# Unused unit-matrix products on TensorE at four places of a hybrid mLSTM/NSA decoder step

## The reference, cut to what matters

```python
h = rmsnorm(x, g_mix)
proj = h @ w_in + b_in
h_a, ... = mlstm_branch(...)            # chunkwise: C_new = decay * C + sum_s ws * k (x) v
o_b, ... = attend(...)                  # NSA: compressed, selected and window branch
gm = sigmoid(g_mrg)
y = gm[..., :D_MODEL] * (h_a @ w_a) + gm[..., D_MODEL:] * (o_b @ w_b)
x = x + y @ w_o
x = x + swiglu(rmsnorm(x, g_ffn), w_ffn_in, w_ffn_out)
```

## Time and profile before

| | |
|---|---|
| time, median of 3 runs | 2207.27 us (2204.72 to 2209.68) |
| time of the profiled execution | 2205.3 us |
| its span, first to last instruction | 2203.3 us |
| mean granted TensorE clock over the span | 0.96 |
| PE busy | 2016.2 us (92%) |
| DVE busy | 1045.0 us (47%) |
| ACT busy | 764.2 us (35%) |
| POOL busy | 527.9 us (24%) |

### The profile page before, as it was taken

The page is one execution under the profiler, slowest core; times in us unless marked ns, Lnnn a source line. Parts: engine busy times, 40 slices in busy tenths (PEclk is TensorE's granted clock), DMA queues, the critical chain, the costliest instruction groups (busy, mean ns, idle before and its releaser), DMA issues. The chain is left out here.

```text
span 2203.3 us, 33142 instructions
## 1 busy us (share of the span) xinstructions
PE 2016.2 (92%) x13796; PEld 1862.3 (85%) x13796; DVE 1045.0 (47%) x1752; ACT 764.2 (35%) x1435; POOL 527.9 (24%) x440
## 2 busy tenths in 40 slices
PE   4999999966888986998899999899999999999997
PEld 3999999855666763665799989899999999999997
DVE  4988863466888874314232343533343323322222
ACT  4233333443766761222222233322222224432212
POOL 2445322203654571222011112111111001111000
PEclk9999999885999986999999999999999999999999
DMA  5465531101000006354433331333323333333332
GB/s 186 126 196 170 158 122 36 40 6 39 1 1 20 1 1 224 112 171 133 153 92 96 88 101 44 94 89 87 96 85 89 96 99 98 100 108 88 87 89 66
DMA packets 258147, 203.11 MB, mean 92 GB/s; under 512 B 20342, under 2 KB 237276, under 8 KB 252687
## 3 DMA queue, kind: packets, MB, share of 16 engines
q1 hardware_dynamic: 246399, 150.92, 23.6%
q0 software_dynamic: 6144, 39.46, 5.2%
q10 hardware_dynamic: 5456, 10.62, 1.5%
HBM read 178.59 MB, written 26.54 MB: 93 GB/s over the span
## 5 line engine op out<-in xcount | busy, mean ns | idle before, releaser
L2933 DVE TENSOR_TENSOR ffn_w_l<-ffn_raw,ffn_w_h 128x1024 fp32r<-128x1024 f32 (+1 forms) x136 | 163.8, 1205 | 273.6 <-ACT ffn_w_h L2866 273.3
L98 PE MATMUL banks<-h_h,ffn_w_l 128*128 128x264 f32 x1408 | 288.3, 286 | 5.5 <-DVE ffn_w_l L2933 5.5
L98 PE MATMUL banks<-h_l,ffn_w_h 128*128 128x264 f32 x1408 | 288.2, 286 | 0.0
L98 PE MATMUL banks<-h_h,ffn_w_h 128*128 128x264 f32 x1408 | 287.9, 286 | 0.0
L2866 ACT CAST ffn_w_h<-ffn_raw 128x1024 fp32r<-128x1024 f32 (+1 forms) x136 | 138.6, 1020 | 332.2 <-PE banks L98 331.1
L98 PEld LDWEIGHTS banks<-h_h,ffn_w_l 128*128 128x128 f32 x1408 | 220.1, 189 | 6.0 <-DVE ffn_w_l L2933 5.8
L98 PEld LDWEIGHTS banks<-h_l,ffn_w_h 128*128 128x128 f32 x1408 | 219.4, 189 | 0.0
L98 PEld LDWEIGHTS banks<-h_h,ffn_w_h 128*128 128x128 f32 x1408 | 219.2, 189 | 0.0
L2854 POOL TENSOR_TENSOR act_l_rest<-ffn_act,act_h 128x528 fp32r<-128x528 f32 x38 | 71.3, 1876 | 377.3 <-ACT act_h L2874 377.3
L674 POOL TENSOR_TENSOR fm_w_l<-fm_raw,fm_w_h 128x512 fp32r<-128x512 f32 x54 | 96.5, 1788 | 218.4 <-ACT fm_w_h L731 218.4
L89 PE MATMUL banks<-fm_hT_h,fm_w_l 128*128 128x352 f32 x648 | 146.8, 335 | 0.5 <-DVE hT_l L863 0.5
(11 more groups left out here) (517 smaller groups left out, 4244.3 us busy)
## 6 DMA issues: line engine op xcount, KB each, us to landing
ffn_raw<-in_w_ffn_in_dram SPq DMA_DIRECT2D x88, 512.0 KB, 3.9
ffn_raw<-in_w_ffn_out_dram SPq DMA_DIRECT2D x32, 512.0 KB, 4.0
fm_raw<-in_w_in_dram SPq DMA_DIRECT2D x44, 256.0 KB, 3.1
early_w_raw<-in_w_in_dram SPq DMA_DIRECT2D x32, 256.0 KB, 2.9
merge_raw<-in_w_in_dram SPq DMA_DIRECT2D x32, 256.0 KB, 2.9
ffn_raw<-in_w_ffn_out_dram SPq DMA_DIRECT2D x16, 384.0 KB, 3.5
hT_copy<-fm_hT_h SPq DMA_DIRECT2D x4, 1056.0 KB, 6.6
hT_copy<-hT_l SPq DMA_DIRECT2D x4, 1056.0 KB, 5.3
```

The lines of the kernel that those rows point to most:

```text
L98: mm = pe.matmul(out[:, bank, 0:cols.stop - cols.start], w[:, kt, :], x[:, cols], start=(first and n == 0), stop=(last and n == 2))
L2933: dve.tensor_tensor(w_l[n % NSPLIT][:, 0:m, :], raw[n % NRAW][:, 0:m, :], w_h[n % NSPLIT][:, 0:m, :].bitcast(F32), ALU.subtract).then_inc( ...
```

## The change

At four places PE is given products of the unit matrix `ident` with itself, 128 x 128 in fp32, whose results in PSUM nobody reads:

- in the mLSTM sample loop four in each of the 8 turns, ahead of the wait for the weighted keys (`s_kws`). The wait for the state update of b - 2 (`s_c`), which stood behind that wait, now stands ahead of the four, since they write the same PSUM banks;
- 16 ahead of PE's first scores in the prompt attention;
- 20 ahead of PE's first block in the merge;
- 12 ahead of PE's first block in the FFN.

That is 80 products in all. No other engine's program changes.

```diff
@@ mLSTM, sample loop @@
                             turn_out(late, ST)
-                        pe.wait_ge(s_kws, c + b + 1)
                         if b > 1:
                             pe.wait_ge(s_c, MH * (S + b - 1))
+                        for _ in range(4):
+                            pe.matmul(ps[:, (DC, BCM)[b % 2], 0:P], k.ident[:], k.ident[:], start=True, stop=True)
+                        pe.wait_ge(s_kws, c + b + 1)
                         for h in range(MH):
@@ stage_nsa_prompt @@
+            for _ in range(16):
+                pe.matmul(ps[:, 7, 0:P], k.ident[:], k.ident[:], start=True, stop=True)
             for u in range(HG):
                 scores_slc(u)
@@ stage_merge @@
+            for _ in range(20):
+                pe.matmul(ps[:, 7, 0:P], k.ident[:], k.ident[:], start=True, stop=True)
             for n, (src, kt0, f) in enumerate(blocks):
@@ stage_ffn @@
+            for _ in range(12):
+                pe.matmul(ps[:, 7, 0:P], k.ident[:], k.ident[:], start=True, stop=True)
             for n, (hf, src, kt0, m, f) in enumerate(blocks):
```

## The result

The changed kernel takes 2222.85 us, the median of four runs (2219.91 to 2226.29), against 2207.1 us before, again of four. The ratio is 1.0074, with a 95% interval of 1.0059 to 1.0089, so the change costs 13 to 20 us. The forecast was 2221 us and "slower". The profiled execution took 2219.91 us with a span of 2218.0, 14.7 us more than the span before.

The account below looks back on a forecast made before the run. The change could gain only through TensorE's clock, in the few stretches at 0.50; PE is busy for most of the span. Loop 12.0, attention 0.2, merge 2.3 and FFN -0.5 gave +14.0 us, 2221 us, range 2211 to 2227.

Parts of the forecast that it names:

- The loop, +12.0 forecast: Sample loop: four products lengthen each of turns 1 to 7 by 1.72 us at half clock, turn 0 free; +12.0 us.
- the first rival: Sample loop: new full-height work brings the clock up in two to four turns; +6 to +10 us, chance 0.16.
- The price from the earlier trace: One unused fp32 product costs 0.22 us at full clock and 0.43 us at half clock.
- the gains of a loop at full clock: Sample loop's lower bound: full clock throughout saves 13.6 us over seven turns, ending the loop 1.6 us sooner.
- the keys were not always ready: Sample loop: keys are made two turns early, so the wait for them is over when PE comes to it.
- The clock in the loop: Sample loop: PEclk stays at 0.50, since 5.96 us of unbroken 32-row products did not bring it back.
- Prompt attention, +0.2 forecast: Prompt attention: 16 products take 6.0 us and delay the scores, following heads run at full clock; net +0.2 us.
- Merge, +2.3 forecast: Merge start: room 1.8 us, 20 products take 6.9 us, blocks start later but at full clock; +2.3 us.
- the sum: Whole kernel: 12.0 + 0.2 + 2.3 - 0.5 = +14.0 us, median 2221 us.
- FFN, -0.5 forecast: FFN start: room 2.4 us, 5 products fast and 7 slow, blocks start at 1400.8; -0.5 us.
- The second and third: Rivals: clock holds through the loop, 2208 us, chance 0.11; also attention's first 13.5 us at full clock, 2202, chance 0.06.

Follow-up runs that it names:

- The loop alone: Only the 32 products of the sample loop, the three starts as before, against the kernel before: ratio 1.0056, +12 us.
- the run with four in the pause: Loop only, four products in each of turns 1 to 4 ahead of the transposes, in PE's pause, against the kernel before: ratio 1.0001.
- The eight-product run: Loop only, 8 products a turn in place of 4, nothing elsewhere, against the kernel before: ratio 1.0080, +18 us.
- the starts alone: Only the 16, 20 and 12 products at the starts of prompt attention, merge and FFN, loop as before, against the kernel before: ratio 1.0012, +2.6 us.
- the run with all pauses: Products only where PE idles: loop, behind the mLSTM's last transpose, attention's opening, both sides of two barriers, against the kernel before: ratio 0.9962, 8 us faster.
- the fitted starts: Products at the three starts only, 8, 4 and 6 in place of 16, 20 and 12, against the kernel before: ratio 0.9995.
- both kernels with all pauses: Products in all PE pauses, ratio 0.9962, and the same with 6 ahead of the mLSTM's last transpose, 8 behind, 15 at the opening, 0.9958, against the kernel before.

## Why the prediction was right

**The loop, +12.0 forecast, +12.5 measured.** The step that carried it was where the products stand: behind the transposes, while PE's pause is ahead of them. The loop alone gives it back on its own (+12.5), and in turns 1 to 4, where there is a pause to move them into, the same four cost nothing ahead of the transposes (loop 35.09 us). That the total fits to 0.5 us is in part luck: two parts were off in size and made up for each other. In turns 1 and 2 the addition is 1.70 us for 1.72. In turn 3 part of the work ran at the full clock, 7.00 us in place of 7.7, the first rival in a small way. In turns 4 to 7 a group of four costs 2.01 us and not 1.72, 1.2 us more in all. Turn 0 was free, as forecast.

The price from the earlier trace rows was that of products among others of as many rows. The waits are not what adds to it: in turns 1 and 2, behind transposes on 128 rows, the group takes 1.84 us (484.51 to 486.35), and only between products on 32 rows 2.01. The same holds for the turn's own products: 2.01 us with 128-row products behind them (496.34 to 498.35 in the run with four in the pause), 1.88 with 32-row ones (489.33 to 491.21), behind the same waits. So each change between 32 and 128 rows costs 0.13 to 0.17 us here. The earlier trace rows held a warning that a group can cost more than the price: 5.96 us for three of them, where it gives 5.2.

Two small slips of the prediction changed nothing: the gains of a loop at full clock add up to 13.5 us and not 13.6, and the keys were not always ready, for before the change PE waited 0.18 us for them in turn 7 (L1254 at 509.44, on DVE's L1368).

**The clock in the loop.** Forecast 0.50, measured 0.54. That it would stay down was argued from the 5.96 us of unbroken 32-row products that had not raised it. The run with 32-row products in the pauses bears this out, for they did not even hold a clock that was up. The eight-product run shows how near the first rival was: with eight, the clock does come up in some turns.

**Prompt attention, +0.2 forecast.** The 16 products took 5.93 us (forecast 6.0), and a head then 1.16 us in place of 1.60:

```profile
528.03 6.17 PE L1772 MATMUL banks<-ident 128*128 128x128 f32 x32 [3.39 <-PEq L3164]
533.96 0.30 PE L1721 MATMUL banks<-keys_hl,queries_hh 128*128 128x128 f32 x1
...
536.50 0.33 PE L1736 MATMUL banks<-keys_hl,queries_hh 128*128 128x128 f32 x1 [0.28 <-DVE row_neg_max L1866]
...
537.66 0.33 PE L1736 MATMUL banks<-keys_hl,queries_hh 128*128 128x128 f32 x1 [0.28 <-DVE row_neg_max L1866]
```

Late start and faster heads cancel: DVE's first factors (L1877 of before) come 10.67 us after the stage's opening, 10.74 before, and 11.07 with the starts alone, so -0.1 and +0.3 around the forecast. With eight products they come at 10.12, sooner than with 16. The +0.8 us of the table lie behind that, and are less than the 2.7 us by which this kernel and the starts alone differ in those stages.

**Merge, +2.3 forecast, +3.8 measured.** The products took 6.43 us (forecast 6.9), and up to the first block on y the stage is 2.2 us longer, as forecast. The remaining 1.6 us come later, behind the first block on y: from there to the FFN's opening it is 112.7 us with the change and 111.1 before. The clock is at half there for twice as long. The stretches at 0.50 around that block, before, with the change, and then in the run with all pauses; the last row is the same place, at full clock, with products on both sides of the two barriers alone:

```profile
1285.10:1288.50 3.40, 2.87 (x9) 2.56 (x9) 3.40 (x2) 0.86 (x2) 3.40 (x2) 0.50 0.04 7
```

```profile
1301.00:1307.80 6.80, 5.45 (x19) 5.00 (x19) 6.80 (x6) 1.07 (x1) 3.89 (x5) 0.50 0.62 191
```

```profile
1276.90:1283.70 6.80, 5.62 (x20) 5.17 (x19) 6.80 (x5) 1.07 (x1) 4.13 (x5) 0.50 0.59 193
```

```profile
1285.00:1296.00 11.00, 7.41 (x44) 6.62 (x44) 11.00 (x9) 2.84 (x5) 6.33 (x5) 1.00 0.50 165
```

PE did 2.6 us more of its work at half clock than before (5.45 against 2.87), which is worth 1.3 of the 1.6 us. All five runs with 112.6 to 112.8 us here (the change, the starts alone, the fitted starts, both kernels with all pauses) have such a stretch of 6.8 us from 1.0 to 1.4 us behind the first block on y on; the six with 111.1 to 111.3 us have one of 3.4 us that begins ahead of the block, or none. Only the run with eight products in the loop fits neither (3.4 us, 112.1). Of the six kernels with products at the merge's start, five have the long stretch, and of the six without none, so the change may well have a part in it. But products there don't decide it alone: the last two rows are of kernels with the same merge program, and these differ by 1.5 us. What puts the half clock there is open; the sum had no such term.

**FFN, -0.5 forecast.** The products took 4.10 us (forecast 4.1), and to the sum of squares it is 10.29 us in place of 10.74, -0.5; to the end -1.0, within the 1.9 us by which the kernels whose FFN is that of before differ there.

**Rivals.** The second and third asked for the clock to survive the pause before turn 1. It did not: PE idled for 4.27 us, and the transposes behind the pause take 1.11 us, as before, and not the 0.66 of full clock. The clock can be held through the loop, but only by products in the pauses: then the kernel becomes faster by 7 us. The Trainium skill's page "TensorE: Matmul & The Clock Gate", section "Why this matters for your kernels", was weighed there; the traces agree with its advice where the pauses themselves are filled with products on 128 rows (clock 1.00, -5.3 us in the loop), while work put beside the pauses leaves them open (0.54, +12.5 us). They don't agree that keeping TensorE busy is enough, for with products on 32 rows it was busy for 37.1 of 37.4 us at 0.54.

## What to carry to other kernels

A product that is to keep TensorE's clock up belongs ahead of the wait at which PE idles, and has to fill the pause: in a burst it only lengthens the chain (+1.7 to 2.0 us in most turns here), and in the pause the same four are free but useless, while eleven on 128 rows bring a turn from 5.97 to 4.58 us. Look first on which side of a stage's barrier the idle time lies; here 5.5 of the 7.35 us of the merge's pause lay ahead of it (from 1084.80 to SP's first DMA of the stage at 1090.31), out of reach of products behind it. And count them at the clock that PE will have when it comes to them, for at half clock they take twice as long (0.43 us in place of 0.22), and twelve behind the mLSTM's last transpose made a barrier 2 us late.

## What the runs showed of the hardware

Products on 32 rows of the array did not hold TensorE's clock even with PE busy for 37.1 of 37.4 us (mean 0.54), where products with the same columns on 128 rows held it at 1.00 with PE busy for 20.2 of 22.1 us. And plain fp32 products at half clock cost 0.43 us each among others of as many rows, but four on 128 rows between groups on 32 rows took 2.01 us, 0.3 more than four times that: each change between 32 and 128 rows added 0.13 to 0.17 us.
